# Moving the scratch area of a two-model forward pass from the end of on-chip memory to its start

## What is computed

```python
# first block, for each of 2 layers
mix = concat(mla_attention, diff_attention, forgetting_attention)(h @ w_in) @ w_out
h = layer_norm(ALPHA * h + mix)
for e in range(16):                       # 16 experts of width 512, each token goes to 2
    y += gate[:, e] * ((silu(h @ w_gate[e]) * (h @ w_up[e])) @ w_down[e])
h = layer_norm(ALPHA * h + y)
# second block, for each of 2 layers
x = x + 0.5 * swiglu(rms_norm(x), wi, wo)         # width 2816
x = x + (ssd_pool_mixer or swa_sink_attention)(rms_norm(x))
x = x + memory_cross_attention(rms_norm(x))
x = x + 0.5 * swiglu(rms_norm(x), wi, wo)
```

## The kernel before, in words

| tile | start before | in a line of 64 | start after | in a line of 64 |
|---|---|---|---|---|
| stage0 | 16,512 | 0 | 204,224 | 0 |
| hi0, hi1, hi2 | 41,088, 49,280, 57,472 | 0 | 93,472, 101,664, 109,856 | 32 |
| lo0, lo1, lo2 | 65,664, 73,856, 82,048 | 0 | 118,048, 126,240, 134,432 | 32 |
| thi, tlo | 90,240, 98,432 | 0 | 142,624, 150,816 | 32 |
| ahi, alo | 106,624, 110,720 | 0 | 159,008, 163,104 | 32 |
| X, gb_ | 114,816, 123,008 | 0 | 167,200, 175,392 | 32 |
| scr, scr_r | 151,840 | 32 | 16,512 | 0 |

## Time and profile before

### The profile page before, as it was taken

The page is one execution under the profiler, slowest core; times in us unless marked ns, Lnnn a source line. Parts: engine busy times, 40 slices in busy tenths (PEclk is TensorE's granted clock), DMA queues, the critical chain, the costliest instruction groups (busy, mean ns, idle before and its releaser), DMA issues.

```text
span 2146.1 us, 28281 instructions
## 1 busy us (share of the span) xinstructions
PE 2063.0 (96%) x10176; PEld 1712.0 (80%) x10176; DVE 1491.2 (69%) x2035; ACT 1214.1 (57%) x1928; POOL 67.8 (3%) x105
## 2 busy tenths in 40 slices
PE   7989999989889999999999999999999999899999
PEld 6777888878767888878887988788888887778887
DVE  7579999987679999987455658555555457665554
ACT  4555777765547777755444665554444445465443
POOL 0001000000010000010000000000000001000000
PEclk9998999999989999999999999999999999999999
DMA  6235999974228999965556444356556656134663
GB/s 252 85 101 187 369 359 352 358 298 141 99 84 322 356 372 357 356 240 193 192 180 197 153 134 148 117 177 185 187 167 205 189 184 198 59 118 160 193 188 108
DMA packets 124200, 446.56 MB, mean 208 GB/s; under 512 B 14320, under 2 KB 15472, under 8 KB 123120
## 3 DMA queue, kind: packets, MB, share of 16 engines
q1 hardware_dynamic: 124048, 444.61, 60.4%
HBM read 443.51 MB, written 1.05 MB: 207 GB/s over the span
## 4 chain that ended last, share of the span: by engine, by line
PE 50%; ACT 2%; DVE 2%; issue 1%; POOL 0%; DVEq 0%; ACTq 0%
PE bank L1271 7%; PE bank L1272 7%; PE bank L1280 7%; PE bank L1304 4%; PE bank L1302 4%; PE bank L1303 4%; PE bank L641 3%; PE bank L642 3%; PE bank L644 3%; PE bank L1250 1%; PE bank L2955 1%; PE bank L2916 1%; PE bank L2957 1%; PE bank L2956 1%; PE bank L2937 1%
## 5 line engine op out<-in xcount | busy, mean ns | idle before, releaser
L597 DVE TENSOR_TENSOR lo<-stage,hi 128x1024 fp32r<-128x1024 f32 (+1 forms) x834 | 970.5, 1206 | 251.4 <-ACT hi L585 195.5
L585 ACT ACTIVATE hi<-stage 128x1024 fp32r<-128x1024 f32 (+1 forms) x834 | 828.0, 1042 | 236.9 <-PE bank L1304 112.8
L1271 PE MATMUL bank<-hi,thi 128*128 128x512 f32 x704 | 278.2, 395 | 0.0
L1272 PE MATMUL bank<-lo,thi 128*128 128x512 f32 x704 | 274.5, 390 | 0.0
L641 PE MATMUL bank<-hi,thi 128*128 128x512 f32 (+3 forms) x584 | 228.2, 391 | 17.0 <-DVE scr L2049 4.5
L642 PE MATMUL bank<-lo,thi 128*128 128x512 f32 (+3 forms) x584 | 222.4, 381 | 0.0
L2573 PE MATMUL bank<-hi,scr_r 128*128 128x512 f32 x512 | 206.5, 403 | 1.4 <-DVE lo L597 1.4
L644 PE MATMUL bank<-hi,tlo 128*128 128x512 f32 (+3 forms) x584 | 206.3, 380 | 0.0
L1280 PE MATMUL bank<-hi,tlo 128*128 128x512 f32 x704 | 202.5, 389 | 0.0
L2574 PE MATMUL bank<-lo,scr_r 128*128 128x512 f32 x512 | 202.1, 395 | 0.0
L2575 PE MATMUL bank<-hi,scr_r 128*128 128x512 f32 x512 | 201.8, 394 | 0.0
(11 more groups left out here) (417 smaller groups left out, 2906.2 us busy)
## 6 DMA issues: line engine op xcount, KB each, us to landing
stage<-in_exp SPq DMA_DIRECT2D x384, 512.0 KB, 5.2
stage<-in_ffn SPq DMA_DIRECT2D x264, 512.0 KB, 4.2
stage<-in_wi_a SPq DMA_DIRECT2D x16, 512.0 KB, 6.1
stage<-in_wi_b SPq DMA_DIRECT2D x16, 512.0 KB, 4.4
stage<-in_mem_wkv SPq DMA_DIRECT2D x16, 512.0 KB, 4.9
stage<-in_xwq SPq DMA_DIRECT2D x16, 512.0 KB, 4.4
stage<-in_xwo SPq DMA_DIRECT2D x16, 512.0 KB, 4.4
stage<-in_ssd_xbc SPq DMA_DIRECT2D x12, 512.0 KB, 3.8
```

The lines of the kernel that those rows point to most:

```text
L585: a.activation(self.hi[i % NR][:, x:y], self.stage[(2 * i + p) % (2 * NS)][:, :y - x], ACT.Copy).then_inc(*c.tick(("hi", i, p), sem="hi"))
L597: v.tensor_tensor(self.lo[i % NR][:, x:y], self.stage[(2 * i + p) % (2 * NS)][:, :y - x], self.hi[i % NR][:, x:y].bitcast(F32), ALU.subtra ...
L1271: t.matmul(out, self.thi[:, xs], hi[:, ws], start=(k == 0), stop=False)
L1272: t.matmul(out, self.thi[:, xs], lo[:, ws], start=False, stop=False)
```

## The change

The scratch tile `scr`, with its second view `scr_r`, is allocated first and not last, and the six staging buffers last and not first. All other tiles keep their order. No instruction, wait, size or DMA changes, on any engine; the order of instructions of each engine is row for row the same.

```diff
-        self.stage = [sb(f"stage{i}", CW // 2) for i in range(2 * NS)]
+        self.scr = sb("scr", SCR)
+        self.scr_r = nc.alloc_sbuf_tensor_at("scr_r", [128, SCR], F32R, offset=nc.sbuf_base - 4 * SCR)
         self.hi = [sb(f"hi{i}", CW, F32R) for i in range(NR)]
         self.lo = [sb(f"lo{i}", CW, F32R) for i in range(NR)]
...
         self.st = sb("st", 288)
         self.small = sb("small", 100)
-        self.scr = sb("scr", SCR)
-        self.scr_r = nc.alloc_sbuf_tensor_at("scr_r", [128, SCR], F32R, offset=nc.sbuf_base - 4 * SCR)
+        self.stage = [sb(f"stage{i}", CW // 2) for i in range(2 * NS)]
```

## The result

The changed kernel takes 2154.4 us (median of 9 runs, 2152.23 to 2158.65) beside 2148.51 us (9 runs, 2145.24 to 2152.06) of the kernel before on the same chip: ratio 1.0029, 95% interval 1.0020 to 1.0038. That is 4.3 to 8.2 us slower, more than the 0.2% that can be told from no change. The forecast was no change. The profiled execution took 2156.18 us, span 2154.4 us.

A forecast was written before the change was run, and what follows sets the result against it. TensorE was taken as the bound: in the long stages, the number of matmuls by their pace. All terms were taken as 0, one deciding term lying between 0 and 40 us, giving 2148.5 us, range 2137 to 2190.

The forecast's parts named there:

- The main stream: 5,616 TensorE matmuls whose two operands move together from 0 to 32: 0 taken, or 38 us if any operand off a line pays.
- that group: Four L2508 at 940.55 us, both operands half a line off: 393 ns median read as no penalty for each operand.
- any operand off a line: Rival for the main stream and L688's kind: one operand off pays once, 38 + 2 us, 2188 us; chance 0.26.
- each pays for itself: Rival for the main stream: each operand off a line pays, 5,616 x 13.4 ns = 75 us, 2224 us; chance 0.07.
- never settles: Rival for the main stream: both operands off keep 393 ns, 4 above 389, 22 us more, 2171 us; chance 0.09.
- VectorE, ScalarE and the staging buffers: Tiles moving on or off a line cost these engines 0; staging buffers stay on a line, DMA cost taken as 0.
- The experts' gate-up: 3 x 512 TensorE matmuls, stationary 32 to 0, moving 0 to 32: half a line apart before and after, 0.
- half a line apart only hurts one way round: Rival: the experts' gate-up settles at 227 ns, 10 us less, 2138 us; chance 0.12.

The follow-up runs named there:

- e3: Kernel before with 32-byte pads ahead of `hi` and `scr`, so all matmul operands stand half a line off: 2143.95 us, ratio 0.9971.
- e4: Kernel before with 32 unused bytes between `lo` and `thi`, moving the main stream's stationary operands and the scratch area: 2171.6 us, ratio 1.0103.
- e1: Kernel before with 32 unused bytes ahead of the scratch area, gate-up distance 224 becoming 0: 2144.34 us, ratio 0.9977.
- e9: Like the kernel before with the scratch area padded to distance 0, plus staging buffers 32 bytes off a 64-byte line: 2146.09 us, ratio 0.9974.
- e7: Kernel before with the main stream's stationary operands 256 bytes away, gate-up kept at distance 0: 2144.92 us, ratio 0.9975.
- e5: Kernel before with the main stream's stationary operands 64 bytes away, gate-up kept at distance 0: 2172.5 us, ratio 1.0123 to the kernel before.
- e6: Kernel before with the main stream's stationary operands 128 bytes away, gate-up kept at distance 0: 2171.3 us, ratio 1.0097.
- e12: Kernel before with a 192-byte pad ahead of the scratch area, giving the gate-up the change's distance 160: 2153.75 us, ratio 1.0018 to the kernel before.
- e2: Changed kernel with 32-byte pads behind the scratch area and ahead of the staging buffers, gate-up distance 128: 2151.71 us, ratio 1.0006 to the kernel before.
- e8: Changed order with 160 unused bytes behind the scratch area, all distances 0: 2143.94 us, ratio 0.9971 to the kernel before.

## Why the prediction was wrong

**The main stream: right.** 0 of the possible 38 + 2 us. L1271 and L1302 kept 389 and 390 ns, and e3 and e4 show why: all operands moved together by 32 bytes cost nothing, one of the two moved alone costs 27 us (e4's 2171.6 less e1's 2144.34, both with the gate-up at 0). The reason the prediction gave, that a penalty for each operand would not let fall back to 393 ns, led the right way, but was thin: worked out from the addresses, the two operands of that group stand a multiple of 256 bytes apart, and its 393 ns, like the 233 ns between its starts, is that of a run that has not settled. Eight matmuls could as well have pointed the other way. The rivals "any operand off a line", "each pays for itself" and "never settles" are ruled out by e3.

**VectorE, ScalarE and the staging buffers: right.** After the change the row of L1349 still reads 691 ns and that of L2674 386 ns, as in the earlier trace rows; e9 moved the staging buffers and lost nothing that can be told.

**The experts' gate-up: the step that failed.** The prediction put it as "half a line apart before and after: 0 by either reading", on a line of 64 bytes taken from the table of starts. The line is 256 bytes (e7 against e5 and e6), and in it the distance went from 224 to 160. Two different distances looked like one because the earlier trace rows were read as "0" and "not 0" alone, and every tile start was reduced to its place in 64 bytes before they were compared. What it costs instead: 0.8 ns (232.94 to 233.76 before rounding) on each of 1,536 gate-up matmuls, 1.3 us.

**The down products behind them: a term that was missing.** They cost more than the gate-up itself: 3.5 ns on each of 744, 2.6 us, although their own operands kept distance 0. Before, they ran at 227 from their first; after, the first nine starts of a run are 231 ns apart on the mean and the next two 227, and e12 brings this about in the order of before, with the same nine values to 1 ns. The sum charged each matmul by its own operands alone. Why a run behind distance 160 starts slow and one behind 224, 128 (e2) or 0 does not was not found.

**The rival "half a line apart only hurts one way round"** had the right place, the gate-up, and the right price for a gate-up that settles: e1 gains 6.5 us in the medians, where the rival asked for 10. It had the wrong condition: what the change gave it was another distance, not 0.

**The size.** The experts' pace gives 3.8 us of the change's 4.3 to 8.2. The change and e12 have the same pace, the intervals of their ratios overlap, and e8 shows the order without the distance at no cost. What is left over is 0.5 to 4.4 us by that sum, and nothing that can be told from e12. The profiled executions point at the stretches at 1.2 GHz (66.2 us before, 73.0 after, 70.2 in e12, 59.4 in e8). The stretch with most of it, the attention of the first block's second layer, in the kernel before and after:

```profile
480.00:650.00 170.00, 153.52 (x867) 125.63 (x866) 120.73 (x250) 87.68 (x204) 14.78 (x28) 0.95 0.34 112
```

```profile
480.00:650.00 170.00, 154.81 (x847) 125.81 (x847) 116.38 (x243) 84.16 (x196) 14.78 (x28) 0.91 0.33 106
```

The granted clock there is 0.95 and 0.91, and e12, with the same gate-up and down rows as the kernel after, had 0.93. One profile each doesn't tell whether the change makes it lower or it differs from one execution to the next. The mean granted clock of the whole span is on record for more of them: 0.9832 over the change's nine runs, 0.9839 to 0.9844 over the 77 runs of the kernel before beside which the experiments were measured. A microsecond at 1.2 GHz counts as half of one at full clock in that mean, so as an estimate 0.0007 to 0.0012 of 2,150 us, 1.5 to 2.6 us, come with the clock, and that would be a good part of what is left. But these are other rounds than the change's own, and in e12, where both were measured together, 0.9834 and 0.9839 can't be told apart. So this part stays open.

On the pages that the prediction weighed: the Trainium skill, page "SBUF — State Buffer", section "Specifications (TRN2)", has lines of 16 bytes, and its section "Who interferes with whom" gives TensorE two independent read ports and has it never wait on anyone. The runs show more than either: with every tile on a multiple of 32 bytes, moving one of the two operands by 32 bytes costs 5.8 ns of 227.4, and moving both by 32 costs nothing.

## What to carry to other kernels

Where TensorE is the bound and loads a new stationary operand for each 512-column matmul, give all operands of matmuls starts that are equal modulo 256 bytes; here that is worth 0.2 to 0.3% beside the kernel before, for a pad of 32 bytes in its order of tiles (e1) or of 160 behind the scratch area in the other (e8), and getting it wrong in the main stream costs 1% at 32, 64 or 128 bytes. Other shapes and types were not tried. Work such places out from addresses, and compare them at full resolution before you reduce them to on and off: two cases that look alike by half a line were two different cases. And charge a changed stage with the stage behind it as well, for the larger half of the loss here lay in matmuls that nothing had been done to.

## What was not expected of the hardware

- The pace of TensorE depends on where the stationary operand starts relative to the moving one, and 256 bytes count as 0: main stream 227.4 ns at 0 and at 256 (e7), 233.2 at 32, 233.3 at 64, 232.6 at 128, 229.1 at 192.
- A run of matmuls can depend on the run ahead of it: the experts' down products at distance 0 take 231.0 ns behind a gate-up at 160, slow for nine starts and settled from the tenth, and 226.7 to 227.4 behind one at 0, 128 or 224.
- Even at distance 0 the gate-up has 228.5 ns and not 226.7: it is broken up more often, and in e1's timeline it first runs 12 matmuls 226 to 227 ns apart, and behind a break by two small L2500 then some 232:

```profile
296.63 0.39 PE L2574 MATMUL bank<-hi,scr_r 128*128 128x512 f32 x1
...
299.12 0.39 PE L2576 MATMUL bank<-hi,scr_r 128*128 128x512 f32 x1
299.35 0.38 PE L2500 MATMUL bank<-const_sb,scr 128*128 128x128 f32 x2
...
299.80 0.40 PE L2575 MATMUL bank<-lo,scr_r 128*128 128x512 f32 x1
...
301.89 0.39 PE L2575 MATMUL bank<-lo,scr_r 128*128 128x512 f32 x1
```

From 299.80 to 301.89 are 9 starts in 2.09 us, 232 ns each, with all operands at distance 0. On the mean of the 54 gate-up runs of e1 behind a break the starts are 234, 233, 235, 225, 231, 235, 228, 232, 231 and then 227 and 227 ns apart. That is, to little over 1 ns, the sequence of the down products after the change. So the distance decides what pace a run can settle at, and what stands ahead of the run decides whether it settles at once or after nine starts. No experiment tried the second by itself, and what in the engine takes nine starts is not known.
